# Last head's order, a norm folded into the following projections, and moved fills in a two-block transformer kernel

## The reference, cut to what matters

```
y   = concat([y_a, y_b]) @ w_out                      # y_b: mLSTM, 4 heads of 256
h   = h + rmsnorm(y, post_g)                          # end of the even mixer
hn  = rmsnorm(h, pre_g)                               # start of the odd mixer
u, v, z = split(hn @ w_in)                            # 3 x 2048
v   = rmsnorm(gelu(v), sg_norm_g)
vs  = causal(w_spatial) applied over 128 tokens, + b_spatial
y   = gelu(u) * vs * silu(z)
h   = h + rmsnorm(y @ w_out, post_g)
```

## Time and profile before

| | |
|---|---|
| runs | 2749.68, 2751.76, 2754.51 us, median 2751.76 |
| profiled execution | 2746.48 us, its span 2744.7 us |
| TensorE | busy 2629.0 us, 96% |
| VectorE | 1515.4 us, 55% |
| ScalarE | 1070.0 us, 39% |
| GpSimd | 872.6 us, 32% |
| HBM read | 239.02 MB, 88 GB/s over the span |
| chain that ended last | TensorE 13% of the span, VectorE 1% |

### The profile page before, as it was taken

The page is one execution under the profiler, slowest core; times in us unless marked ns, Lnnn a source line. Parts: engine busy times, 40 slices in busy tenths (PEclk is TensorE's granted clock), DMA queues, the critical chain, the costliest instruction groups (busy, mean ns, idle before and its releaser), DMA issues. The chain is left out here.

```text
span 2744.7 us, 38228 instructions
## 1 busy us (share of the span) xinstructions
PE 2629.0 (96%) x14758; PEld 2131.1 (78%) x14758; DVE 1515.4 (55%) x2863; ACT 1070.0 (39%) x1862; POOL 872.6 (32%) x650
## 2 busy tenths in 40 slices
PE   6899999999999999999899999999999999999997
PEld 4787786788888888766668888777768887688886
DVE  4434444687777778556654444544456544415444
ACT  4444545422222223565542232354444434442222
POOL 1211121243333333021134444333334343244443
PEclk8999999999999999999999999999999999999999
DMA  6323333233333332010012322222212222222221
GB/s 243 116 85 95 114 100 102 83 116 107 107 107 107 107 107 79 25 47 32 32 62 92 102 97 92 84 74 77 77 47 91 72 77 77 78 92 92 92 92 62
DMA packets 69652, 243.02 MB, mean 89 GB/s; under 512 B 11780, under 2 KB 29700, under 8 KB 49288
## 3 DMA queue, kind: packets, MB, share of 16 engines
q1 hardware_dynamic: 69512, 241.15, 26.0%
HBM read 239.02 MB, written 2.10 MB: 88 GB/s over the span
## 5 line engine op out<-in xcount | busy, mean ns | idle before, releaser
L248 POOL TENSOR_TENSOR w_lo<-w_raw,w_hi 128x512 fp32r<-128x512 f32 x616 | 826.4, 1373 | 1777.1 <-ACT w_hi L241 602.8
L287 PE MATMUL bank<-u_hi,w_hi 128*128 128x512 f32 (+1 forms) x1952 | 731.9, 375 | 12.4 <-DVE u_lo L547 5.0
L289 PE MATMUL bank<-u_hi,w_lo 128*128 128x512 f32 (+1 forms) x1952 | 719.2, 368 | 0.0
L288 PE MATMUL bank<-u_lo,w_hi 128*128 128x512 f32 (+1 forms) x1952 | 718.4, 368 | 0.0
L287 PEld LDWEIGHTS bank<-u_hi,w_hi 128*128 128x128 f32 x1952 | 368.7, 189 | 82.9 <-issue 16.2
L288 PEld LDWEIGHTS bank<-u_lo,w_hi 128*128 128x128 f32 x1952 | 368.8, 189 | 62.2 <-issue 2.5
L289 PEld LDWEIGHTS bank<-u_hi,w_lo 128*128 128x128 f32 x1952 | 368.3, 189 | 62.4
L1052 DVE SCALAR_TENSOR_TENSOR resid<-bank,mod,resid 128x512 f32<-128x512 f32 (+1 forms) x384 | 241.9, 657 | 140.6 <-PE bank L289 136.2
L287 PE MATMUL bank<-hid_hi,w_hi 128*128 128x512 f32 (+1 forms) x768 | 275.5, 359 | 0.0
L289 PE MATMUL bank<-hid_hi,w_lo 128*128 128x512 f32 (+1 forms) x768 | 273.0, 355 | 0.0
L288 PE MATMUL bank<-hid_lo,w_hi 128*128 128x512 f32 (+1 forms) x768 | 272.1, 354 | 0.0
(11 more groups left out here) (399 smaller groups left out, 3852.6 us busy)
## 6 DMA issues: line engine op xcount, KB each, us to landing
w_raw<-stream SPq DMA_DIRECT2D x150, 1024.0 KB, 4.9
w_raw<-stream SPq DMA_DIRECT2D x56, 512.0 KB, 4.4
ada_ring<-stream SPq DMA_DIRECT2D x48, 512.0 KB, 4.7
bias<-bias SPq DMA_DIRECT2D x192, 64.0 KB, 2.2
ada_more<-stream SPq DMA_DIRECT2D x6, 1024.0 KB, 12.9
resid<-h SPq DMA_DIRECT2D x2, 1536.0 KB, 9.4
w_raw<-stream SPq DMA_DIRECT2D x8, 256.0 KB, 3.8
out<-resid SPq DMA_DIRECT2D x8, 256.0 KB, 2.0
```

The source lines that it names most:

```text
L248: ins = eng.tensor_tensor(m.wl[:, s, w], m.raw[:, s, w], m.wh[:, s, w].bitcast(F32), ALU.subtract)
L287: pe.matmul(out, lh, rh, start=start, stop=False)
L288: pe.matmul(out, lh, rl, start=False, stop=False)
L289: return pe.matmul(out, ll, rh, start=False, stop=stop)
```

## The change

1. mLSTM, last head only. TensorE runs `outputs` ahead of half 1 of z, three tiles of the head before's output projection ahead of the sum of squares and five behind it (before: five and three). `outputs` waits for each state by itself. Silu of z is computed by halves: half 0 before the denominator, half 1 after the numerators. ScalarE's split of the last fill goes behind the squares and half 1's inverse.
2. End of the mLSTM stage. The low part of the next stage's first chunk goes from GpSimd to VectorE, in quarters between the last adds; the low part of the second chunk goes to the next stage, in quarters within `add_post`.
3. Odd stage. u is no longer multiplied by rstd before it is split: the high part is gain times h, the low part its remainder. So the v products start while the residual is being formed. GpSimd adds six squares; TensorE sums three tiles after the first v group, and turns rstd into columns in the second group. v's GELU takes rstd as a scale by token (a column), u and z are multiplied by rstd by VectorE in reading their banks; GELU and tanh then read SBUF.
4. The split of chunk 2 goes between the sixth and seventh square, that of chunk 3 ahead of the root; chunk 3 is loaded when the second chunk's low part is done. Fillers: 3 + 3 become 4.

The core of the diff:

```diff
 # order, mLSTM
-            order += [("R", i), ("M", i), ("W", i), ("z", i, 0)] + [("u", i, c) for c in range(3)] + [("z", i, 1)]
-            order += [("den", i), ("num", i, 0), ("num", i, 1)]
-            sum_at = 5 if i + 1 == H else KT
+            outs = [("den", i), ("num", i, 0), ("num", i, 1)]
+            order += [("R", i), ("M", i), ("W", i), ("z", i, 0)] + [("u", i, c) for c in range(3)]
+            order += [("z", i, 1)] + outs if i + 1 < H else outs + [("z", i, 1)]
+            sum_at = 3 if i + 1 == H else KT
 # gpsimd, mLSTM
-                coming.low(pool, 0)
                 post.add(pool)
 # scalar, mLSTM
                     z_gate(i, 0)
+                    if i + 1 == H:
+                        inverse_half(0)
                     z_gate(i, 1)
...
+                    else:
+                        squares(i)
+                        inverse_half(1)
                         high(fill["z", i] + 2)
 # vector, mLSTM
+                    if i + 1 == H:
+                        z_added(0)
                     states(i)
...
+                        z_multiplied(0)
                     denominator(i)
                     numerator(i)
...
+                    if i + 1 == H:
+                        z_added(1)
+                        add(i - 1, 0)
+                        z_multiplied(1)
                     output_norm(i)
...
                 for k in range(KT):
                     add(H - 1, k)
-                coming.low(dve, 1)
+                    if 1 <= k < 5:
+                        coming.low_quarter(dve, 0, k - 1)
 # tensor, mLSTM
-                    project_half("z", i, 1, ("z", i, 1))
-                    outputs(i)
+                    else:
+                        outputs(i)
+                        project_half("z", i, 1, ("z", i, 1))
...
-                        project_out(i - 1, range(5))
+                        project_out(i - 1, range(3))
                         sums(i)
-                        project_out(i - 1, range(5, KT))
+                        project_out(i - 1, range(3, KT))
 # sync, odd
+                    if n == 3:
+                        sp.wait_ge(*first_fills.lo.at(2))
 # gpsimd, odd
+                pool.wait_ge(*squared.at(6))
+                for k in range(1, 6):
+                    if k > 1:
+                        pool.wait_ge(*sq_added.at(k - 1))
+                    pool.tensor_tensor(sq[0], sq[0], sq[k], ALU.add).then_inc(sq_added.sem)
 # scalar, odd
                 for k in range(KT):
                     act.wait_ge(*post_h.at(k + 1))
+                    act.activation(m.uh[:, k, 0:LAT], m.h[:, k, 0:LAT], ACT.Copy,
+                                   scale=col(m, "pre1")[:, k:k + 1]).then_inc(high_u.sem)
                     act.activation(sq[k], m.h[:, k, 0:LAT], ACT.Square).then_inc(squared.sem)
+                    if k == 5:
+                        high(2)
+                high(3)
...
-                        act.activation(v[:, c, 2 * h * GD:2 * (h + 1) * GD], lin.out(n),
-                                       ACT.Gelu_apprx_tanh).then_inc(lin.free[n % 8].sem)
+                        act.activation(v[:, c, 2 * h * GD:2 * (h + 1) * GD], lin.out(n), ACT.Gelu_apprx_tanh,
+                                       scale=rc[:, c:c + 1]).then_inc(lin.free[n % 8].sem)
...
-                        act.activation(gu[:, j, :], lin.out(n), ACT.Gelu_apprx_tanh).then_inc(lin.free[n % 8].sem)
+                        act.wait_ge(*lin.read(use["u", i, j]))
+                        act.activation(gu[:, j, :], gu[:, j, :], ACT.Gelu_apprx_tanh).then_inc(u_gelu.sem)
 # vector, odd
+                def add_post(stats, gain):
+                    def split_low(k):
+                        dve.wait_ge(*high_u.at(k + 1))
+                        dve.scalar_tensor_tensor(out=m.ul[:, k, 0:LAT], in0=m.h[:, k, 0:LAT],
+                                                 scalar=col(m, "pre1")[:, k:k + 1],
+                                                 in1=m.uh[:, k, 0:LAT].bitcast(F32), op0=ALU.mult,
+                                                 op1=ALU.subtract).then_inc(low_u.sem)
+                    dve.wait_ge(*stats.rooted())
+                    for k in range(KT + 1):
+                        if k < KT:
...
+                            dve.wait_ge(*post_y.at(k + 1))
+                            h = m.h[:, k, 0:LAT]
+                            dve.tensor_tensor(h, h, m.y[:, k, :], ALU.add).then_inc(post_h.sem)
+                        if k:
+                            split_low(k - 1)
+                        if 1 <= k < 5:
+                            first_fills.low_quarter(dve, 1, k - 1)
...
+                        dve.tensor_tensor(gu[:, j, :], lin.out(n), rstd[:, :], ALU.mult).then_inc(lin.free[n % 8].sem)
...
+                    dve.tensor_tensor(zs[:, j, :], lin.out(n), rstd[:, :], ALU.mult).then_inc(lin.free[n % 8].sem)
...
                 for i in range(G):
+                    u_by_rstd(i)
                     spatial(i)
                     if i + 1 < G:
                         stage(i + 1)
+                    z_by_rstd(i, 0)
+                    z_by_rstd(i, 1)
                     gate(i)
 # tensor, odd
+                def total_squares():
+                    pe.wait_ge(*sq_added.at(5))
+                    pe.wait_ge(*squared.at(KT))
+                    for x, k in enumerate((0, 6, 7)):
+                        ins = pe.matmul(lin.out(n), cst(m, "ones"), sq[k], start=(x == 0), stop=(x == 2))
...
-                keep_busy(pe, m, lin.out(use["sum",]), 3)
-                for k in range(KT):
-                    pe.wait_ge(*squared.at(k + 1))
-                    ins = pe.matmul(lin.out(use["sum",]), cst(m, "ones"), sq[k], start=(k == 0), stop=(k == KT - 1))
-                ins.then_inc(lin_done.sem)
-                keep_busy(pe, m, lin.out(use["v", 0, 0]), 3)
+                keep_busy(pe, m, lin.out(use["sum",]), 4)
```

More of the change, by code:

```diff
@@ L3487, in z_silu, with z_added, z_multiplied @@
                             lin.free[n % 8].sem)
+                def z_added(j):
+                    dve.wait_ge(*z_exp.at(2 * H - 1 + j))
+                    dve.tensor_scalar(sz[:, j, :], sz[:, j, :], BIG, 1.0, ALU.min, ALU.add).then_inc(z_add.sem)
+                def z_multiplied(j):
+                    n = use["z", H - 1, j]
+                    dve.wait_ge(*z_inv.at(H + j))
+                    dve.scalar_tensor_tensor(out=sz[:, j, :], in0=sz[:, j, :], scalar=col(m, "ml_g")[:, j:j + 1],
+                                             in1=lin.out(n), op0=ALU.mult, op1=ALU.mult).then_inc(lin.free[n % 8].sem)
                 def masked(i):
@@ L3883, in odd_stage @@
         index = {"v": lambda g: g, "u": lambda i: G + 3 * i, "z": lambda i: G + 3 * i + 1, "wo": lambda i: G + 3 * i + 2}
-        order = [("sum",)] + [("v", h, c) for h in range(G // 2) for c in range(NC)]
+        order = [("v", 0, c) for c in range(NC)] + [("sum",), ("columns",)]
+        order += [("v", h, c) for h in range(1, G // 2) for c in range(NC)]
         for i in range(G):
@@ new lines, in u_by_rstd, with z_by_rstd @@
+                def u_by_rstd(i):
+                    if i:
+                        dve.wait_ge(*gated.at(i))
+                    for j in range(2):
+                        n = use["u", i, j]
+                        dve.wait_ge(*lin.ready(n))
+                        dve.tensor_tensor(gu[:, j, :], lin.out(n), rstd[:, :], ALU.mult).then_inc(lin.free[n % 8].sem)
+                def z_by_rstd(i, j):
+                    n = use["z", i, j]
+                    if i:
+                        dve.wait_ge(*z_gated.at(2 * i + j - 1))
+                    dve.wait_ge(*lin.ready(n))
+                    dve.tensor_tensor(zs[:, j, :], lin.out(n), rstd[:, :], ALU.mult).then_inc(lin.free[n % 8].sem)
@@ L4055, in gate @@
                     for j in range(2):
-                        n = use["z", i, j]
                         dve.wait_ge(*z_act.at(2 * i + j + 1))
-                        dve.scalar_tensor_tensor(out=sz[:, j, :], in0=sz[:, j, :], scalar=1.0, in1=lin.out(n),
-                                                 op0=ALU.add, op1=ALU.mult).then_inc(lin.free[n % 8].sem)
-                        dve.wait_ge(*lin.read(n))
+                        dve.scalar_tensor_tensor(out=sz[:, j, :], in0=sz[:, j, :], scalar=1.0, in1=zs[:, j, :],
+                                                 op0=ALU.add, op1=ALU.mult).then_inc(z_gated.sem)
+                        dve.wait_ge(*z_gated.at(2 * i + j + 1))
                         dve.wait_ge(*gated.at(i + 1))
@@ L4076, in low @@
                     dve.tensor_tensor(yl[i % 2], y4, yh[i % 2].bitcast(F32), ALU.subtract).then_inc(y_low.sem)
-                post(post0, "post0", 0)
-                dve.wait_ge(*rooted.at(1))
-                scale(0)
-                for k in range(KT):
-                    if k + 1 < KT:
-                        scale(k + 1)
-                    dve.wait_ge(*high_u.at(k + 1))
```

(8 more changed lines are left out.)

88 lines of the change are left out of this document (55 added, 33 removed).

## The result

The changed kernel takes 2733.98 us (median of 5 runs, 2732.39 to 2735.99) against 2751.76 us (5 runs, 2745.28 to 2754.51) before: ratio 0.9942, 95% interval 0.9932 to 0.9953. The changed kernel's profiled execution spans 2732.2 us (time 2733.98 us), 12.5 us less than before.

The account below looks back on a forecast made before the run. TensorE bounds the kernel, so only its 24.5 us handover hole and four waits can pay. Gains 3.4 + 2.3 + 2.4 = 8.1 us take 2746.5 to 2738.4 profiled, 2743.7 as median (5.3 higher); range 2736.5 to 2749.0.

Parts of the forecast that it names:

- part 3: Odd stage, norm joined to the projection: second group of products starts at S + 35.3 instead of S + 37.7, gain 2.4 us.
- Part 1: Last head of the mLSTM stage: three TensorE waits of 3.7 us go, 0.3 us charged for states, gain 3.4 us.
- Rival B: Last head's chain is late again, part 1 worth 0.4 us; gain about 5 us, 2746.7 us; chance 0.17.
- Part 2: Handover at the mLSTM stage's end: barrier 6.3 instead of 8.56 us after the last product, gain 2.3 us.
- S + 30.1 + 1.7 + 2.8 + 0.7: Odd stage, from barrier S: first 96 products with waits, clock fall, three sums, four transposes; second group at S + 35.3.
- Waits 4.5 in the sum: Odd stage, first group: TensorE waits 1.4 us at the sixth tile, 2.9 at the seventh; 96 products end S + 30.1.
- 1.03 us a meeting: Odd stage: alternative price of a VectorE and GpSimd collision (1.37 less 0.34), giving S + 28.4 for the 96 products.
- S + 18.4: Odd stage: time of the seventh low part of u after barrier S if GpSimd's adds hold nothing up.
- S + 28.4: Odd stage: end of the first 96 products at 1.03 us per meeting; S + 30.1 was taken instead.
- Part 4: The eight units: VectorE's added operations are covered, slack 2.4 us falls to 1 to 1.6, cost 0.
- Rival C: Eight units: z chain grows beyond its 2.4 us slack, TensorE waits in seven units; slower, 2757.7 us; chance 0.06.
- Rival A: First group: GpSimd and VectorE do not collide, or VectorE gets two turns to one; gain 14.9, 2736.9 us; chance 0.25.

Follow-up runs that it names:

- the second profile of the kernel before: the kernel before, profiled again without an edit: 2752.49 us (one run).
- kernels 1 and 5: 1: kernel before with only the last head's new order, 2748.71 us; 5: that plus the first fill's low part in quarters on VectorE, 2744.48 us.
- kernel 7: changed kernel with GpSimd's five adds of squares held until VectorE has written the last low part of u: 2737.19 us.
- kernel 9: changed kernel with GpSimd's first add of squares one tile sooner, after the fifth square instead of the sixth: 2741.06 us.
- kernel 8: changed kernel with the second fill's low part back in the mLSTM stage, low part of u between scaling and add, one filler fewer: 2734.26 us.
- kernel 3: changed kernel without the last head's new order: 2743.15 us.
- kernel 6: changed kernel with the product of z's second half by rstd made three times more in each unit: 2741.89 us.
- kernels 4, 8, 12: 4 and, again, 12: changed kernel with the second fill's low part back at the mLSTM stage's end, 2734.40 and 2734.26 us; kernel 8 has its own line.
- kernel 2: kernel before with only the first fill's low part moved from GpSimd to VectorE, in quarters: 2750.79 us.
- changed again: the changed kernel, profiled and timed a second time without an edit: 2736.07 us.

## Why the prediction was wrong

The direction and the mechanism of each part held; the sum was 5.5 us too small against the stretch, and 4.3 of these lie in part 3: its waits in the first group and its fall of the clock were sized too high.

**Part 1** (3.4 us; measured 4.46). The three waits went. Two sizes were off. The wait that I charged for the states, 0.3, isn't there: from the updates to the next product it is 1.93 us now (2300.74 to 2302.67); before it was 1.64 to a product that itself took 0.29 us more than its pitch, which is the same. And the list of waits shows less than an idle costs: the wait of 2.06 us above stands between starts 2362.64 and 2365.09, 2.45 us where the pitch is 0.23, so 2.2, and the product behind it takes 0.34 to the next start instead of 0.23: 2.3 us in all. For three waits that is some 0.7 us. The Trainium skill (Perfetto Trace Analysis, "Tensor Engine Instruction") says that the end of a matmul in a profile is computed and not observed; the rows agree, 0.39 us long at a pitch of 0.23. Rival B, the late head chain, did not come about, though VectorE's last low part was drawn out to 2.4 us from 1.23.

**Part 2** (2.3; measured 2.39). The new handover is as forecast: wait 1.35 as in the MLP stage's 1.44, sum at 2.81, barrier 6.17 behind the last product's end (6.3 forecast). That the gain fits to 0.1 us is luck in part: 1.7 of it is the clock's fall at the old handover, which the second profile of the kernel before had in the head. There the last product starts at 2346.36 and the barrier is at 2354.46, so against it part 2 is worth 1.5 us and part 1 more. What the text didn't see is that part 1 without part 2 loses 1.3 us again (kernels 1 and 5).

**Part 3** (2.4; measured 6.75). The step that failed is the sum S + 30.1 + 1.7 + 2.8 + 0.7, by its first two terms. Measured, term by term:
- First group without waits, S + 25.6: S + 25.4 (start 3.59 behind the barrier).
- Waits 4.5 in the sum: 2.6 (24.38 us from 2346.31 to 2370.69, less 21.8). The mechanism was right, the number of meetings and their price were not: four, at 1.0 us each (4.1 us by kernel 7), instead of five at 1.2. VectorE's add that starts with GpSimd's first slips through at 0.69 us, and a pair has a pitch of 1.7 us (2358.17 to 2363.28 in three), not 1.9. The prediction had this price among its two ends, 1.03 us a meeting from the earlier trace rows, and set it aside. Put on the seventh low part's S + 18.4 it gives the end of the group at S + 28.0 with four meetings, which is what was measured (2370.69 against the barrier at 2342.72), and S + 29.0 with five; the S + 28.4 that stands beside it fits neither. The sixth low part was to come at S + 18.8 and came at S + 17.2, just before TensorE wanted it. One meeting more would have made two waits of it, as kernel 9 shows: this count stood on an edge, and a single value was taken from it. How near the edge was, kernel 8 shows too: there VectorE's add starts 0.1 us behind GpSimd's first (2359.43 and 2359.32) and is drawn out to 1.78 us.
- Clock 1.7: 0. One wait of 2.06 us was left, and the clock did not fall, nor did it in the second profile (2.04). That is no merit of the change: it fell behind the same wait in kernel 3, and in 6 of the 13 such idles counted in the last section.
- Sum 2.8, transposes 0.7: 2.6 (2370.69 to 2373.50 less one pitch) and 0.4 (2376.04 to 2376.70 less one pitch).

**Part 4** (0). Right: from the second on the eight mixings stand 34.4 us apart in both kernels (the first gap is 23.6 in both), and the slack left is 1.15 us where 1 to 1.6 was forecast (kernel 6). Rival C would have needed 1.1 us more in the chain to cost anything.

**Rival A** had the collision wrong and the size nearly right (14.9). GpSimd and VectorE do collide; only three fifths of the loss and no clock came with it. Its chance of 0.25 was fair for its reason, but the sum in between, with one wait, was given no place of its own.

**The base.** Between the profiled executions 12.5 us were won, between the medians 17.8, in the stretch 13.6. The first profile of the kernel before had the earliest start of the last head of all 14 executions, so that its own time, 2746.5, lies at the low end. That is no effect of the change, and the stretch is free of it. The forecast's step of 5.3 us from the profiled execution to the median did no harm: 13.6 us from 2751.8 would be 2738.2, inside the range, and the median of the runs lies 4.2 us below that. The second set of runs won 15.7 us (2751.78 to 2736.07). No run shows a cause for what goes beyond 13.6; it is within what the intervals allow.

**Open:** whether the early low part (kernels 4, 8, 12) is truly faster, and what makes executions differ by up to 8 us ahead of the last head.

## What to carry to other kernels

Count the meetings of VectorE and GpSimd in a chain that TensorE follows closely, and price each at a GpSimd operation less the part that overlaps (here 1.3 less 0.3 us); where one more or less decides about a wait, forecast both. A reordering that brings TensorE to a point sooner pays only if the queue that feeds this point is freed with it. Compare two kernels over the stretch that starts just ahead of the edit, not over the span, when the difference is less than what executions vary by.

## What was not expected of the hardware

Whether the clock falls behind an idle of some 2 us is not settled by the idle's length. Between 2285 and 2400 us ten of the profiles hold 13 idles of TensorE of 1.97 to 3.30 us, each behind products at full speed, and behind six of them the granted clock fell to 0.50, which is the 1.2 GHz level, for 3 to 4 us: behind 1.97 (kernel 9), 2.02 and 2.06 (kernel 3), 2.02 (before, second profile), 2.04 (before) and 3.30 (kernel 1), but not behind 2.02 (kernel 2), 2.04 (before, in the head; changed again; kernel 6), 2.06 (changed; kernel 7) and 2.49 (before, second profile). In this part of the run it never fell behind an idle of 1.51 us or less. A fall costs 1.7 us: the six products of the sum take 4.51 us with it and 2.81 without. So I would price an idle of 2 us at its length, 0.3 for the restart and about half of 1.7. The Trainium skill (TensorE: Matmul & The Clock Gate, "Part 1: The HAM clock gate") says that the gate judges activity on a count of its own that no kernel starts anew, so that the point of change varies from run to run; the same waits with and without a fall agree, though no run here shows the count.

The 1.51 us are no safe length elsewhere. Between 1244 and 1316 us each of the 14 profiles holds two idles of 1.42 to 1.44 us among the small products of the sliding-window attention, and behind 18 of these 28 the clock fell, and in kernel 7 it fell once in the mLSTM stage behind 0.49 us, also among small products. A line of TensorE's timeline and a stretch (length, busy times, granted clock) of the kernel before, then of kernel 7:

```profile
1244.43 0.70 PE L2530 MATMUL bank<-k_rotated,q_rotated 64*128 64x256 f32 x2 [1.43 <-DVE y_lo L2369]
1246.30:1249.60 3.30, 3.30 (x13) 2.91 (x12) 2.11 (x6) 1.76 (x4) 3.30 (x3) 0.50 0.00 0
```
```profile
2107.55 0.50 PE L287 MATMUL bank<-u_hi,w_hi 128*128 128x512 f32 x1 [0.49 <-POOL w_lo L248]
2107.90:2111.20 3.30, 3.30 (x9) 2.58 (x8) 2.04 (x4) 2.79 (x7) 3.30 (x3) 0.50 0.79 271
```

So the count of 6 in 13 holds for idles behind full 128x512 products, and what else makes the clock fall is open.
